# Hybrid decoder trunk: GpSimd issues the converting transfer of the next weight pair ahead of both subtracts of the present pair

## Chip, core and metric

The kernel runs on one core of one Trainium2 chip. The time is device microseconds of one execution. A profiled execution also gives a trace, whose span is a little shorter than the execution's time.

## What is computed

Two decoder layers act on x, 512 tokens by 2048 features, in float32. The part that matters here is the two large products of each layer:

```python
h = rms_norm(x, norm_g)
p = jnp.einsum('btd,dp->btp', h, w_in)          # 2048 x 7192
ya, yb, yc, yd = four mixers of slices of p     # GLA, window, differential, gated delta
y = jnp.concatenate([ya, yb, yc, yd], axis=-1)
return x + jnp.einsum('btm,md->btd', y, w_out)  # 2048 x 2048
```

The mixers are causal attention of four kinds, with 4 heads each, and a SiLU gate on each.

## The kernel before

**Split float32.** TensorE multiplies in a reduced float32 format (fp32r). To keep accuracy both factors are split into a high half (rounded to fp32r) and a low half (what is left), and three products are added: high by high, high by low, low by high (line 549).

**The weight stream.** All weights lie in DRAM as one stream of slices, each 128 rows by 512 columns, in the order in which they are used: 288 per layer, 576 in all. The trace and this text call the work on one slice a step (the code: kt). A step is 12 matmuls of 128x512: 4 accumulators by 3 products. Two slices make a pair; pair g holds steps 2g and 2g+1. There are 144 pairs per layer (`PAIRS`).

**Who makes what.** For each pair:

- SP's queue loads the raw float32 pair, 512 KB, into `w_raw`, 3 buffers deep (`RAW`, line 432). It may overwrite a buffer once both subtracts of the pair three before are done (line 431).
- GpSimd's queue loads the same pair a second time with a transfer that converts float32 to fp32r, into `w_hi`, 3 buffers deep (`HI`, `high_halves`, lines 477 to 482). It may overwrite a buffer once TensorE has done both steps of the pair three before (line 480). For the first 8 pairs (`FIRST_HI`) ScalarE makes the high halves instead, from `w_raw`.
- GpSimd subtracts, `w_lo = w_raw - w_hi`, one instruction for each step (line 506), into a ring of 4 `w_lo` buffers (`RING`). It waits for the buffer's last reader: the subtract of step n needs step n-4 done (line 505).
- TensorE waits before step n for its subtract, by the count `w_ready` (line 537), and counts `kt_done` after it (line 552). `kt_done` starts at 4.

GpSimd is one queue in order. Its loop (lines 484 to 509) takes for pair g: the wait for the raw pair, the wait for the high halves, the even subtract, then `high_halves(g + 1)` with its own wait, then the odd subtract. In pair 10 of the first layer it first converts masks (`masks`), and in the seventh pair of each layer it first scales some small weights (`small_weights`).

**TensorE's order.** `project` (line 525) runs the steps of one block of output columns and interleaves pieces of the mixers, so some steps follow each other directly and between others there are small matmuls. ScalarE and VectorE empty the accumulators (lines 1064, 1573, 1940) and do the mixers' elementwise work. At the end of a layer x, 4 MB, is written to DRAM in four transfers of 1 MB from ScalarE's queue (line 1472), while ScalarE (line 1084) and VectorE (lines 1521 to 1541) already prepare x for the next layer.

Of the kernel before, what the change touches and what calls it, by code (L numbers as in the profile page):

```python
# [16 lines left out]
DEPTH, SEQ, D_MODEL = 2, 512, 2048  # L17
# [22 lines left out]
PAIRS = LAYER_KTS // 2  # L40
RAW, HI, RING = 3, 3, 4
FIRST_HI = KT // 2
# [169 lines left out]
def hybrid_trunk(nc, x, wstream, wsmall, pcol, prow, wlr, cf, masks, out, rows):  # L212
    ctx = ExitStack()
    with ctx:
# [34 lines left out]
        def slot(n):  # L249
            return slots[:, n - FIRST_SLOT]  # L250
# [171 lines left out]
        @block.sync  # L422
        def _(sp):
            def x_in(n):
                k = X_PIECES[n]
                k = slice(k.start, k.stop)
                sp.dma_start(xT[:, k], x.rearrange("(k p) n -> p k n", p=P)[:, k]).then_inc(xin[n], 16)

            def weights(i):
                if i >= RAW:  # L430
                    sp.wait_ge(w_ready, 2 * (i - RAW) + 2)
                sp.dma_start(w_raw[:, i % RAW].rearrange("p a n -> p (a n)"),
                             wstream[i:i + 1].rearrange("a p n -> p (a n)")).then_inc(raw_in[i % RAW], 16)

            x_in(0)
            weights(0)
            x_in(1)
            weights(1)
            x_in(2)
            weights(2)  # L440
            x_in(3)
            for l in range(DEPTH):
                for i in range(PAIRS):
                    if l * PAIRS + i >= RAW:
                        weights(l * PAIRS + i)
                    if l == 0 and i in (RAW, RAW + 2):
                        x_in(4 + (i - RAW) // 2)
                    if i == RAW:
                        sp.wait_ge(ws_ready, l + 1)
                        if l:  # L450
                            sp.wait_ge(S_PE.sem, S_PE.at(l - 1, "small"))
                        sp.dma_start(ws[:, :], wsmall[l:l + 1].rearrange("a p n -> p (a n)")).then_inc(ws_in, 16)


        @block.gpsimd
        def _(pool):

            pool.sem_inc(ws_ready, 1)
            pool.memset(zeros[:, :], 0.0).then_inc(zeros_done, 1)

            def masks():

                pool.wait_ge(masks_in, 16)
                pool.wait_ge(consts_in, 16)
                pool.tensor_copy(mask_sb[:, 0:masks_n], slot(3).rearrange("p a b -> p (a b)")[:, 0:masks_n]) \
                    .then_inc(masks_done, 1)
                pool.tensor_copy(m_upto, upto).then_inc(masks_done, 1)

            def small_weights(l):

                each = ws[:, :].rearrange("p (k c) -> p k c", c=SM)
                pool.wait_ge(ws_in, l * 16 + 16)
                pool.wait_ge(norm_in, 16)
                pool.tensor_tensor(each, each, pcol_all[:, l, 0:KT].unsqueeze(2).broadcast_to([P, KT, SM]), ALU.mult) \
                    .then_inc(ws_ready, 1)

            def high_halves(g):

                if g >= HI:
                    pool.wait_ge(kt_done, RING + 2 * (g - HI) + 2)  # L480
                pool.dma_start(w_hi[:, g % HI].rearrange("p a n -> p (a n)"),  # L481
                               wstream[g:g + 1].rearrange("a p n -> p (a n)")).then_inc(hi_in[g % HI], 16)

            for l in range(DEPTH):
                for i in range(PAIRS):
                    g = l * PAIRS + i
                    if i == 10 and l == 0:
                        masks()
                    if i == 6:
                        small_weights(l)  # L490

                    pool.wait_ge(raw_in[g % RAW], g // RAW * 16 + 16)
                    if g >= FIRST_HI:
                        pool.wait_ge(hi_in[g % HI], len(range(FIRST_HI + (g - FIRST_HI) % HI, g + 1, HI)) * 16)
                    for k in range(2):
                        n = 2 * g + k

                        if n == 0:
                            continue
                        if n == 1:  # L500

                            pool.wait_ge(w_ready, 1)
                        if g < FIRST_HI:
                            pool.wait_ge(hi_made, n + 1)
                        pool.wait_ge(kt_done, n + 1)
                        pool.tensor_tensor(w_lo[:, n % RING], w_raw[:, g % RAW, k], w_hi[:, g % HI, k].bitcast(F32),  # L506
                                           ALU.subtract).then_inc(w_ready, 1)
                        if k == 0 and FIRST_HI <= g + 1 < DEPTH * PAIRS:
                            high_halves(g + 1)


        @block.tensor
# [1610 lines left out]
```

## Time and profile before

| | |
|---|---|
| median of 3 runs | 1834.73 us (1832.11 to 1838.42) |
| profiled execution | 1838.2 us |
| its span in the trace | 1836.1 us |
| TensorE matmul busy | 1817.9 us, 99% |
| GpSimd busy | 922.5 us, 50% |
| VectorE, ScalarE busy | 793.4 us, 511.2 us |
| moved by DMA | 324.98 MB, mean 177 GB/s |
| granted TensorE clock | 0.999 of full |

A busy share is an average over stages. What GpSimd's order of work is worth shows in where TensorE waits for a subtract, and in how far ahead of TensorE the subtracts end elsewhere.

### The profile page before, as it was taken

Reading aid. Unit: us, or ns where it says so; the run is one execution under the profiler, and the core shown is the slowest. Engines: PE = TensorE matmul, PEld = TensorE weight load, DVE = VectorE, ACT = ScalarE, POOL = GpSimd, SP = SyncE. Lnnn points to the kernel's source line nnn. Section 1 sums busy time; section 2 is a strip of 40 time slices with the busy share of each in tenths; the row PEclk is TensorE's granted clock in tenths of the full one; section 3 lists DMA queues with packets and bytes.
Section 4 is the critical chain, followed back from the end, with each engine's and each line's share of the span. In section 5 each row is a group of like instructions: output and inputs, shape, how many; then the busy total and the mean of one; then the engine's idle time right before and its main releaser. Section 6 shows DMA issues by size and latency. Waiting matters only on the chain. (4 is left out here: it accounts for less than half of the span.)

```text
span 1836.1 us, 23457 instructions
## 1 busy us (share of the span) xinstructions
PE 1817.9 (99%) x9462; PEld 1493.9 (81%) x9462; DVE 793.4 (43%) x1631; ACT 511.2 (28%) x991; POOL 922.5 (50%) x864
## 2 busy tenths in 40 slices
PE   8999999999999999999999999999999999999999
PEld 7788888888888888788877888888888888887887
DVE  7546634622111453643534476255311124436342
ACT  6212214022222543322312131140222225433220
POOL 5555544545555444445465555445455554444454
PEclk9999999999999999999999999999999999999999
DMA  7466554655555547455766665546555565474556
GB/s 276 144 191 209 169 161 138 185 151 171 176 171 179 162 146 240 139 158 173 242 207 183 188 205 171 159 142 182 156 170 178 161 180 164 139 242 134 161 173 206
DMA packets 94507, 324.98 MB, mean 177 GB/s; under 512 B 10144, under 2 KB 10688, under 8 KB 94144
## 3 DMA queue, kind: packets, MB, share of 16 engines
q1 hardware_dynamic: 43904, 155.73, 27.6%
q0 software_dynamic: 40320, 146.82, 27.1%
q10 hardware_dynamic: 10176, 20.94, 3.2%
q8 instruction: 74, 1.21, 0.3%
q14 instruction: 33, 0.27, 0.0%
HBM read 315.05 MB, written 8.40 MB: 176 GB/s over the span
## 5 line engine op out<-in xcount | busy, mean ns | idle before, releaser
L506 POOL TENSOR_TENSOR w_lo<-w_raw,w_hi 128x512 fp32r<-128x512 f32 x575 | 762.4, 1326 | 654.3 <-DMA w_hi<-in_wstream 471.4
L549 PE MATMUL acc<-w_hi,actT_hi 128*128 128x512 f32 x1408 | 561.8, 399 | 5.9 <-ACT slots L1064 5.9
L549 PE MATMUL acc<-w_hi,actT_lo 128*128 128x512 f32 x1408 | 549.2, 390 | 0.0
L549 PE MATMUL acc<-w_lo,actT_hi 128*128 128x512 f32 x1408 | 548.5, 390 | 0.0
L549 PE MATMUL acc<-actT_hi,w_hi 128*128 128x512 f32 x896 | 359.2, 401 | 6.8 <-DVE actT_lo L1521 3.2
L549 PE MATMUL acc<-actT_hi,w_lo 128*128 128x512 f32 x896 | 350.1, 391 | 0.0
L549 PE MATMUL acc<-actT_lo,w_hi 128*128 128x512 f32 x896 | 349.8, 390 | 0.0
L549 PEld LDWEIGHTS acc<-w_hi,actT_hi 128*128 128x128 f32 x1408 | 264.6, 188 | 62.3 <-ACT slots L1064 7.6
L549 PEld LDWEIGHTS acc<-w_hi,actT_lo 128*128 128x128 f32 x1408 | 264.3, 188 | 56.1
L549 PEld LDWEIGHTS acc<-w_lo,actT_hi 128*128 128x128 f32 x1408 | 264.7, 188 | 51.5
L481 POOL DMA_DIRECT2D w_hi<-in_wstream x280 | 159.2, 568 | 246.9 <-PE acc L549 242.7
L549 PEld LDWEIGHTS acc<-actT_hi,w_hi 128*128 128x128 f32 x896 | 168.6, 188 | 56.4 <-issue 18.9
L549 PEld LDWEIGHTS acc<-actT_hi,w_lo 128*128 128x128 f32 x896 | 168.6, 188 | 36.3
L549 PEld LDWEIGHTS acc<-actT_lo,w_hi 128*128 128x128 f32 x896 | 168.9, 189 | 32.6 <-issue 0.5
L1064 ACT ACTIVATE slots<-acc,xr 128x512 f32<-128x512 f32 x56 | 37.9, 690 | 172.1 <-PE acc L549 172.1
L1592 DVE SCALAR_TENSOR_TENSOR slots<-slots,pcol_all 128x511 f32<-128x511 f32 (+2 forms) x72 | 82.8, 1155 | 1.7
L1940 DVE TENSOR_TENSOR slots<-acc,slots 128x512 f32<-128x512 f32 x64 | 43.1, 690 | 87.9 <-PE acc L549 87.9
L1573 DVE TENSOR_TENSOR slots<-acc,slots 128x512 f32<-128x512 f32 x24 | 15.7, 688 | 131.9 <-PE acc L549 90.6
L1832 DVE SCALAR_TENSOR_TENSOR slots<-mix,slots 128x256 f32<-128x256 f32 x8 | 3.4, 424 | 133.1 <-ACT slots L1302 133.1
L598 PEld LDWEIGHTS mix<-slots 128*128 128x128 f32 x400 | 48.5, 191 | 2.0
L598 PE MATMUL mix<-slots 128*128 128x128 f32 x400 | 49.0, 275 | 0.0
L1931 DVE SCALAR_TENSOR_TENSOR actT_lo<-mix,pcol_all,actT_hi 128x512 fp32r<-128x512 f32 x32 | 22.4, 746 | 42.2 <-ACT actT_hi L1396 42.2
(270 smaller groups left out, 1558.7 us busy)
## 6 DMA issues: line engine op xcount, KB each, us to landing
w_raw<-in_wstream SPq DMA_DIRECT2D x288, 512.0 KB, 4.4
w_hi<-in_wstream POOLq DMA_DIRECT2D x280, 512.0 KB, 3.8
out_x<-slots ACTq DMA_DIRECT2D x7, 1024.0 KB, 7.5
slots<-in_x ACTq DMA_DIRECT2D x1, 4096.0 KB, 20.7
slots<-out_x ACTq DMA_DIRECT2D x1, 4096.0 KB, 18.4
slots<-in_x SPq DMA_DIRECT2D x3, 1024.0 KB, 12.8
slots<-rows ACTq DMA_DIRECT2D x2, 1024.0 KB, 6.0
out_x<-slots ACTq DMA_DIRECT2D x4, 256.0 KB, 2.1
```

The lines of the kernel that those rows point to most:

```text
L481: pool.dma_start(w_hi[:, g % HI].rearrange("p a n -> p (a n)"), wstream[g:g + 1].rearrange("a p n -> p (a n)")).then_inc(hi_in[g % HI], 16)
L506: pool.tensor_tensor(w_lo[:, n % RING], w_raw[:, g % RAW, k], w_hi[:, g % HI, k].bitcast(F32), ALU.subtract).then_inc(w_ready, 1)
L549: last = nc.tensor.matmul(acc[b][:, :], lhsT, rhs, start=(k == 0 and i == 0), stop=(k == kts - 1 and i == 2))
L598: last = nc.tensor.matmul(mh[bank][:, h], lhsT[:, h], rhs[:, h], start=True, stop=True)
L1064: nc.scalar.activation(slot(SLOT[c])[:, b], acc[b][:, :], ACT.Copy, scale=r) \
L1573: dve.tensor_tensor(slot(SLOT[c])[:, b], acc[b][:, :], rrow, ALU.mult).then_inc(acc_free, 1)
L1592: dve.scalar_tensor_tensor(dst[:, d:], src[:, 0:SEQ - d], tap[i], dst[:, d:], ALU.mult, ALU.add).then_inc(CONV_DVE.sem, CONV_DVE.one(f"{c} ...
L1832: dve.scalar_tensor_tensor(V["G"], mix[1][:, 0:256], 0.0, V["T0"], ALU.min, ALU.subtract) \
L1931: dve.scalar_tensor_tensor(actT_lo[:, k], mix[k % 4][:, :], pcv(l, PC["y"] + k), actT_hi[:, k].bitcast(F32), ALU.mult, ALU.subtract) \
L1940: dve.tensor_tensor(xs, acc[b][:, :], xs, ALU.add).then_inc(acc_free, 1)
```

## The change

The call that issues the converting transfer of pair g+1 moves from between the two subtracts of pair g to the front of the pair, ahead of the waits for the raw pair and the high halves of pair g. The function called is the same; its condition is the same but for `k == 0`, which has no meaning outside the inner loop.

```diff
                     if i == 6:
                         small_weights(l)
 
+                    if FIRST_HI <= g + 1 < DEPTH * PAIRS:
+                        high_halves(g + 1)
                     pool.wait_ge(raw_in[g % RAW], g // RAW * 16 + 16)
                     if g >= FIRST_HI:
                         pool.wait_ge(hi_in[g % HI], len(range(FIRST_HI + (g - FIRST_HI) % HI, g + 1, HI)) * 16)
...
                         pool.wait_ge(kt_done, n + 1)
                         pool.tensor_tensor(w_lo[:, n % RING], w_raw[:, g % RAW, k], w_hi[:, g % HI, k].bitcast(F32),
                                            ALU.subtract).then_inc(w_ready, 1)
-                        if k == 0 and FIRST_HI <= g + 1 < DEPTH * PAIRS:
-                            high_halves(g + 1)
```

## Rows read from the trace of the kernel before

**Rows 1.** The page: span, busy time of TensorE, and one line of its DMA issues.
```profile
span 1836.1 us, 23457 instructions
...
PE 1817.9 (99%) x9462; PEld 1493.9 (81%) x9462; DVE 793.4 (43%) x1631; ACT 511.2 (28%) x991; POOL 922.5 (50%) x864
...
w_raw<-in_wstream SPq DMA_DIRECT2D x288, 512.0 KB, 4.4
```

**Rows 2.** Waits of TensorE: who waited for whom, us in total, times, longest.
```profile
PE acc L549 <- ACT slots L1064: 5.9, 4, 1.7
PE acc L549 <- DVE actT_lo L1521: 3.2, 1, 3.2
PE acc L549 <- POOL w_lo L506: 2.5, 2, 1.6
```

**Rows 3.** Waits of GpSimd, same columns.
```profile
POOL w_lo L506 <- DMA w_hi<-in_wstream: 471.4, 222, 7.4
```

**Rows 4.** Lines 481 (issue) and 506 (subtract): duration min/median/max ns; landing of 481.
```profile
L481 POOL DMA_DIRECT2D w_hi<-in_wstream x280: 567/567/720, 39.9 to 1817.8; - x140
...
DMA to landing us min/median/max: 3.6/3.8/9.2
...
L506 POOL TENSOR_TENSOR w_lo<-w_raw,w_hi x575: 1263/1296/2627, 6.7 to 1823.0; 128x512 fp32r<-128x512 f32 x192
```

**Rows 5.** Timeline of GpSimd, first issue and steady stretch: start us, us, what, [idle before].
```profile
39.87 0.72 POOL L481 DMA_DIRECT2D w_hi<-in_wstream  x1
...
89.47 0.57 POOL L481 DMA_DIRECT2D w_hi<-in_wstream  x1 [0.24 <-PE acc L549]
90.06 1.30 POOL L506 TENSOR_TENSOR w_lo<-w_raw,w_hi 128x512 fp32r<-128x512 f32 x1
93.43 1.28 POOL L506 TENSOR_TENSOR w_lo<-w_raw,w_hi 128x512 fp32r<-128x512 f32 x1 [2.07 <-DMA w_hi<-in_wstream]
```

**Rows 6.** Timeline of TensorE, first matmul of steps 26 and 28.
```profile
89.01 0.39 PE L549 MATMUL acc<-actT_hi,w_hi 128*128 128x512 f32 x1
...
94.45 0.39 PE L549 MATMUL acc<-actT_hi,w_hi 128*128 128x512 f32 x1
```

**Rows 7.** Timeline of GpSimd at the layer boundary.
```profile
912.34 0.57 POOL L481 DMA_DIRECT2D w_hi<-in_wstream  x1
...
918.79 1.30 POOL L506 TENSOR_TENSOR w_lo<-w_raw,w_hi 128x512 fp32r<-128x512 f32 x1 [4.55 <-issue]
920.02 0.57 POOL L481 DMA_DIRECT2D w_hi<-in_wstream  x1
...
924.85 1.89 POOL L506 TENSOR_TENSOR w_lo<-w_raw,w_hi 128x512 fp32r<-128x512 f32 x1 [2.92 <-issue]
926.68 0.57 POOL L481 DMA_DIRECT2D w_hi<-in_wstream  x1
...
931.41 2.63 POOL L506 TENSOR_TENSOR w_lo<-w_raw,w_hi 128x512 fp32r<-128x512 f32 x1 [2.84 <-issue]
933.99 0.57 POOL L481 DMA_DIRECT2D w_hi<-in_wstream  x1
```

**Rows 8.** Timeline of TensorE there: last of step 287, first of 290, 292, 298.
```profile
919.67 0.39 PE L549 MATMUL acc<-actT_hi,w_lo 128*128 128x512 f32 x1
...
926.88 0.47 PE L549 MATMUL acc<-actT_hi,w_hi 128*128 128x512 f32 x1 [0.97 <-POOL w_lo L506]
...
934.19 0.47 PE L549 MATMUL acc<-actT_hi,w_hi 128*128 128x512 f32 x1 [1.58 <-POOL w_lo L506]
...
950.95 0.39 PE L549 MATMUL acc<-actT_hi,w_hi 128*128 128x512 f32 x1
```

**Rows 9.** Timeline of GpSimd around the longest landing.
```profile
705.82 0.57 POOL L481 DMA_DIRECT2D w_hi<-in_wstream  x1 [1.56 <-PE acc L549]
...
715.08 1.29 POOL L506 TENSOR_TENSOR w_lo<-w_raw,w_hi 128x512 fp32r<-128x512 f32 x1 [7.38 <-DMA w_hi<-in_wstream]
```

**Rows 10.** Busy time by window: the last columns are clock, DMA share, GB/s.
```profile
926.00:932.00 6.00, 5.12 (x23) 4.24 (x24) 5.97 (x7) 1.25 (x1) 3.14 (x4) 1.00 0.95 346
```

**Rows 11.** Timeline of VectorE at the boundary: one addition, twice.
```profile
915.96 0.69 DVE L1539 TENSOR_TENSOR slots<-slots 128x512 f32<-128x512 f32 x1
...
925.64 1.64 DVE L1539 TENSOR_TENSOR slots<-slots 128x512 f32<-128x512 f32 x1
```

## The prediction

> **What bounds the kernel now.** I read the busy shares first. TensorE is busy 1817.9 of the 1836.1 us span [rows 1]. No transfer and no other engine can be worth more than the 18 us that are left, unless it stretches TensorE's own work. So the next view is what TensorE waits for [rows 2]: ScalarE's copies out of the accumulators 5.9 us in 4 waits, VectorE's low half of x 3.2 us in one (the start, where x is still arriving), and GpSimd's `w_lo` 2.5 us in 2 waits. Only the last kind is touched by the change. GpSimd itself looks badly held up: its subtracts wait 471.4 us for the `w_hi` transfer [rows 3]. The question is how much of that reaches TensorE.
>
> Sizes: one issue of the converting transfer holds GpSimd 0.57 us, it lands after 3.8 us in the median and 9.2 us at most, and a subtract takes 1.30 us in the median and 2.63 at most [rows 4]. Call one 128x2048 slice of weights a step; TensorE takes 2g and 2g+1 from pair g. In a stretch without other work a pair takes 94.45 - 89.01 = 5.44 us of TensorE, a step 2.72 [rows 6].
>
> **The loop of before.** In such a stretch GpSimd issues the transfer at 89.47, 0.46 us after TensorE began a pair (89.01), subtracts the odd half at 90.06, idles about 2 us, and starts the next even subtract at 93.43 [rows 5, 6]. Issue to subtract is 3.96 us; with 1.28 us for the subtract, 5.24 us are gone, and only behind this subtract may the next transfer be issued. The loop (issue, landing, even subtract, next issue) is serial and has 5.44 - 5.24 = 0.2 us to spare. Any landing over about 4 us makes GpSimd fall behind by the excess. What protects TensorE is the ring of four `w_lo` buffers, a lead that takes several slow transfers to use up.
>
> Between the two layers that happens. The issues come at 912.34, 920.02, 926.68 and 933.99, thus 7.7, 6.7 and 7.3 us apart where TensorE wants 5.44; one landing takes 6.45 us (912.34 to 918.79), and one subtract takes 2.63 [rows 7]. TensorE then starts within 0.15 us of the end of an even subtract: at 926.88 and 934.19 after idles of 0.97 and 1.58 us [rows 8]. Those are the 2.5 us of [rows 2]; smaller hesitations and slower first matmuls after each wait are not in that figure. From the last matmul before step 288 (919.67) to the first of step 298 (950.95) pass 31.28 us; ten steps and one matmul pitch of 0.23 at full pace are 27.43. The loss there is 3.85 us.
>
> **The change, part by part.**
>
> *Moved: 280 issues.* None is added or removed; GpSimd still spends 280 x 0.57 us on them. The wait that comes with the issue of pair g+1 asks for step 2g-3 to be done. This is exactly what the odd subtract of pair g asks for. So where GpSimd is on time the transfer leaves at the same moment as before, 0.46 us after TensorE starts step 2g-2, and lands no earlier. The gain can only be where GpSimd was late.
>
> *Moved behind that wait: the even subtract.* It needed only step 2g-4; now it starts a step later. New timetable from the start of step 2g-2: issue at 0.46, even subtract 1.05 to 2.35, odd subtract to 3.65. TensorE needs the even one at 5.44, so 3.1 us are spare in place of a lead of two to three steps; the odd one is needed at 8.16, with 4.5 spare. With the longest subtract seen, 2.63 [rows 4], the even one still ends at 3.7. Cost: none, covered by TensorE's two steps. If that cover were gone, every microsecond over would be paid per pair.
>
> *Removed: the serial loop.* The transfer of pair g now has from 0.46 after step 2g-4 to about 1.05 after step 2g-2, thus 6.0 us, before it delays GpSimd at all, and until 10.88 - 0.46 - 1.30 = 9.1 us before TensorE waits. The layer boundary's 6.45 is under that by 2.7 us, and still by 1.3 with the 2.63 us subtract. The only landings of 9.2 us are near 705.82, where GpSimd idles 7.38 [rows 9], and the same stretch of the second layer; TensorE has mixer matmuls between its steps there and did not wait for `w_lo` before. There the timing is the same or better, since the following issue no longer stands behind the late one. Gain: between the 2.5 us that the waits list [rows 2] and the 3.85 us of elapsed time; I take the elapsed time, because the slow restarts go with the waits.
>
> *SP's queue.* The next raw load is released by the odd subtract, which ends 1.3 us later than before (3.65 in place of 2.35). It takes 4.4 us in the median [rows 1], so it lands at 8.1, and is first read three pairs later, at 16.32 + 1.05. Nothing waits.
>
> *Start, masks, small weights.* The first moved transfer was issued at 39.87 with GpSimd busy right before it [rows 5]; now it comes before the subtracts of steps 14 and 15. TensorE waits there for x (the 3.2 us of [rows 2]), so step 14 has some 6 us in hand. The masks and the scaling of the small weights stay ahead of the issue; the latter, in pair 150, falls into the 1.8 us that GpSimd has free per pair (5.44 - 3.65). No cost.
>
> *Bandwidth.* In the boundary stretch two `w_hi` transfers may now be in flight. The weight streams at full pace ask for 2 x 512 KB per 5.44 us, 193 GB/s. In the worst 6 us the engines were 95% busy at 346 GB/s [rows 10]. A load landing a little later costs nothing until 9.1 us.
>
> **Sum.** -3.85 us, rounded -3.9. The profiled execution was 1838.2 us, span 1836.1; it becomes 1834.3. It was 3.5 us above the median of the three runs; against that median, 1834.73, the forecast is 1830.9, or 0.21% less. A measurement of this kernel tells about 0.3% (5.5 us) from no change; the three runs of before alone span 0.34%.
>
> **Rivals.**
>
> A. *The time is not kept.* TensorE arrives earlier and then waits as much longer for ScalarE or VectorE, where it already waits 5.9 us [rows 2]. For: those waits exist in the second layer. Against: ScalarE and VectorE get their work from the accumulators, so they move with TensorE. Time 1834.7, chance 0.14. A program whose order makes no difference at all falls here too.
>
> B. *Back-to-back subtracts hold VectorE.* The same VectorE addition takes 0.69 us at 915.96 and 1.64 at 925.64, where it lies beside a subtract; that subtract is slow as well [rows 7, 11]. Before, two subtracts were separated by the issue and the landing; now they form one block of 2.6 us, and a VectorE addition behind it could wait 1.3 us more. It matters where TensorE waits for such a chain: 4 waits on ScalarE and about one more. 5 x 1.3 = 6.5, so 1830.9 + 6.5 = 1837.4. Against: the number of overlaps does not grow, only their grouping, and TensorE hides nearly all. Chance 0.08. The Trainium skill, "SBUF — State Buffer", section "SBUF: two separate sides", speaks against the change here: VectorE and GpSimd share a port pair that one instruction locks whole. By that rule the long times are one engine waiting out the other's instruction, and the time would be B's 1837.4; by the rows it is 1830.9, because few such waits end at TensorE.
>
> C. *Slower.* In the boundary the second `w_hi` transfer in flight takes bandwidth from the first, and landings double, 2 x 6.45 = 12.9. Then two pairs take 0.46 + 12.9 + 1.30 = 14.66 us, 7.33 per pair, 1.89 over TensorE's pace, for the 8 pairs in which the four write-backs of x run: 15.1 us. 1830.9 + 15.1 = 1846.0. It decides only from a landing of 9.1 us. For: 95% busy engines in one stretch [rows 10]. Against: the issues stay tied to TensorE's steps, so total demand rises by no more than the recovered stall. Chance 0.04.
>
> **Numbers.** The forecast has 0.74. Its 0.21% lies near the 0.3% bound, so measurement scatter puts about a fifth of it beyond: faster 0.15. A and B lie within the bound; C and scatter of B give slower 0.06; same 0.79. The range reaches from 1827.0 (forecast less scatter) through A to B, 1837.5; C is left out.
>
> **What would show it.** Right: no TensorE wait on `w_lo` between 915 and 950; steps 288 to 298 in 27.4 to 27.6 us; GpSimd in steady stretches as issue, subtract, subtract, with issues still 0.46 us after TensorE's step; its idle mostly on TensorE and no longer on the transfer; median landing still near 3.8. Wrong: even subtracts ending less than 1 us before their step, TensorE's waits on ScalarE or VectorE grown by what left `w_lo` (A), longer VectorE additions (B), landings over 9 us at the boundary (C).

## The result, and the profile after

The change made the kernel slower: 1850.48 us (median of 6, 1848.9 to 1853.63) against 1835.6 us (1832.11 to 1840.27, 6 runs). The ratio is 1.0081, with a 95% interval of 1.0066 to 1.0096. The forecast was 1830.9 with a range up to 1837.5. One of the eleven executions of run 11 below took 2012.46 us at a granted clock of 0.851; the ratio given there leaves it out.

The page of the changed kernel. In line 508, the subtract, the last number is GpSimd's idle time ahead of it:

```profile
span 1851.5 us, 23457 instructions
...
PE 1822.0 (98%) x9462; PEld 1494.5 (81%) x9462; DVE 844.8 (46%) x1631; ACT 511.4 (28%) x991; POOL 902.4 (49%) x864
...
L508 POOL TENSOR_TENSOR w_lo<-w_raw,w_hi 128x512 fp32r<-128x512 f32 x575 | 739.5, 1311 | 28.7 <-issue 8.7
```

TensorE's work is the same to 4 us, and GpSimd waits 1.5 us for its transfer ahead of a subtract, in place of 471.4 [rows 3]. But VectorE, whose program nobody touched, is busy 51 us longer than in [rows 1]. What TensorE waits for, against [rows 2]:

```profile
PE mix L719 <- DVE halves L1837: 8.4, 8, 1.0
PE acc L549 <- ACT slots L1064: 5.9, 4, 1.7
PE mix L592 <- DVE slots L1677: 3.6, 1, 3.6
PE mix L712 <- DVE slots L1669: 1.8, 2, 0.9
...
PE mix L948 <- DVE slots L1541: 1.4, 1, 1.4
PE mix L865 <- DVE slots L2021: 1.3, 2, 0.7
```

The wait on `w_lo` is gone and the one on ScalarE is unchanged. All that is new is waits for VectorE, at matmuls of the mixers and, at the start, at those that sum the squares of x (line 948). Its instructions by line, first before and then after (count | busy us, mean ns):

```profile
L1592 DVE SCALAR_TENSOR_TENSOR slots<-slots,pcol_all 128x511 f32<-128x511 f32 (+2 forms) x72 | 82.8, 1155 | 1.7
...
L1837 DVE TENSOR_TENSOR halves<-slots,halves 128x256 fp32r<-128x256 f32 x8 | 14.7, 1841 | 0.3
...
L1634 DVE TENSOR_TENSOR glog<-glog,stat 128x16 f32<-128x16 f32 x2 | 0.4, 176 | 0.1
```

```profile
L1592 DVE SCALAR_TENSOR_TENSOR slots<-slots,pcol_all 128x511 f32<-128x511 f32 (+2 forms) x72 | 97.6, 1360 | 1.7
...
L1837 DVE TENSOR_TENSOR halves<-slots,halves 128x256 fp32r<-128x256 f32 x8 | 24.5, 3056 | 0.3
...
L1634 DVE TENSOR_TENSOR glog<-glog,stat 128x16 f32<-128x16 f32 x2 | 6.0, 3024 | 0.1
```

A subtraction of 16 columns went from 0.18 to 3.02 us. It does not compute longer; it is held. The timeline shows by what. Line 1837 makes the low half of the logs in the second mixer (gated linear attention), and TensorE's line 719 needs it. Before, and then after, first GpSimd's rows and then VectorE's:

```profile
420.33 0.57 POOL L481 DMA_DIRECT2D w_hi<-in_wstream  x1 [0.83 <-PE acc L549]
420.92 1.30 POOL L506 TENSOR_TENSOR w_lo<-w_raw,w_hi 128x512 fp32r<-128x512 f32 x1
...
420.69 1.83 DVE L1837 TENSOR_TENSOR halves<-slots,halves 128x256 fp32r<-128x256 f32 x1
```

```profile
425.17 0.57 POOL L481 DMA_DIRECT2D w_hi<-in_wstream  x1 [3.99 <-PE acc L549]
425.76 2.52 POOL L508 TENSOR_TENSOR w_lo<-w_raw,w_hi 128x512 fp32r<-128x512 f32 x2
...
425.52 3.06 DVE L1837 TENSOR_TENSOR halves<-slots,halves 128x256 fp32r<-128x256 f32 x1
```

Before, line 1837 ends 0.3 us after one subtract (422.52 against 422.22); after, 0.3 us after two (428.58 against 428.28). VectorE already lost one subtract here in the kernel before. But it ended in time for TensorE in seven tiles of eight. In the eighth (at 1478.38) the even subtract came late and held the copy of line 1835 ahead of it as well (1.08 us for 0.29), and TensorE waited 0.7 us.

At the start the same thing happens once. VectorE's addition of line 1541 took 0.69 us before (at 46.53). After, it lies beside two subtracts, and the matmuls of line 948, ahead of step 15, wait for it:

```profile
45.86 2.52 POOL L508 TENSOR_TENSOR w_lo<-w_raw,w_hi 128x512 fp32r<-128x512 f32 x2
...
45.56 3.38 DVE L1541 TENSOR_TENSOR slots<-slots 128x512 f32<-128x512 f32 x1
```

The steps of the two traces can be laid beside each other: the start of each step's first matmul after, less that before, and the steps at which this difference changes.

| stretch | change, us |
|---|---|
| start, to step 13 | -5.05 |
| steps 15, 16 (line 948) | +3.25 |
| step 59, behind the convolutions | +5.35 |
| steps 131, 133, 149, 165, 181 and 419, 421, 437, 453, 469 (gated linear attention) | +11.3 |
| steps 196, 484 (window attention) | +1.1 |
| steps 235, 252, 523, 540 (differential attention) | +2.9 |
| steps 288 to 296, layer boundary | -3.4 |
| sum | +15.4 |

This is the difference of the spans, 1851.5 - 1836.1. The first row belongs to the execution of before: TensorE waited 3.2 us there [rows 2]. The boundary run (run 11), with the same order at the start, lost only 0.8 us in place of 5.0 between steps 11 and 14.

Three of these losses are larger than the wait in them, because behind the wait the granted TensorE clock was half of full, 1.2 in place of 2.4 GHz. The rows have TensorE's busy time first and the granted clock third from the end: first before (behind the wait of 3.2 us), then twice after (behind the waits of 1.4 us at line 948 and of 3.6 us at step 59):

```profile
42.80:46.20 3.40, 3.40 (x8) 2.70 (x9) 3.37 (x5) 0.88 (x1) 0.00 (x0) 0.50 0.81 264
...
49.60:53.00 3.40, 3.40 (x10) 2.17 (x10) 0.00 (x0) 0.66 (x2) 0.00 (x0) 0.51 0.37 142
182.70:186.10 3.40, 3.40 (x13) 2.91 (x12) 1.39 (x5) 3.16 (x7) 0.00 (x0) 0.51 0.44 154
```

3.4 us at half the clock are 1.7 us of work not done. The +5.35 of step 59 is thus a wait of 3.6 us and 1.7 us of clock. No such stretch follows the waits of about 1.2 us in gated linear attention.

The boundary went as forecast: the last matmul before step 288 and the first of step 298, 27.42 us apart (31.28 in [rows 8]). These 3.9 us include small drifts that the table's row does not count.

```profile
931.52 0.39 PE L549 MATMUL acc<-actT_hi,w_lo 128*128 128x512 f32 x1
...
958.94 0.39 PE L549 MATMUL acc<-actT_hi,w_hi 128*128 128x512 f32 x1
```

So the question for the experiments is about the 23.9 us that the other rows add: is it that the subtracts are joined, where they lie, or the transfers?

### The profile page after: what moved, and what is told of

It reads as the page before. It is cut to its first block, busy times and chain, and to the rows that moved or that the text cites. A ratio compares the mean times of both kernels' runs of the same rounds, so it can differ in the third digit from the quotient of the medians.

```text
span 1851.5 us, 23457 instructions
## 1 busy us (share of the span) xinstructions
PE 1822.0 (98%) x9462; PEld 1494.5 (81%) x9462; DVE 844.8 (46%) x1631; ACT 511.4 (28%) x991; POOL 902.4 (49%) x864
## 4 chain that ended last, share of the span: by engine, by line
PE 88%; DVE 6%; ACT 4%; DMA 1%; issue 0%; ACTq 0%; SPq 0%; DVEq 0%
PE acc L549 75%; PE mix L598 2%; DVE halves L1837 1%; DVE slots L1592 1%; DMA w_raw<-in_wstream 1%; ACT slots L1064 1%; PE mix L855 1%; PE mix L965 1%; PE mix L784 1%; PE mix L809 1%; PE mix L874 1%; ACT L1302 1%; PE mix L592 1%; DMA slots<-rows 0%; DVE slots L1669 0%
## 5 line engine op out<-in xcount | busy, mean ns | idle before, releaser
L508 POOL TENSOR_TENSOR w_lo<-w_raw,w_hi 128x512 fp32r<-128x512 f32 x575 | 739.5, 1311 | 28.7 <-issue 8.7
L1592 DVE SCALAR_TENSOR_TENSOR slots<-slots,pcol_all 128x511 f32<-128x511 f32 (+2 forms) x72 | 97.6, 1360 | 1.7
L1164 ACT ACTIVATE general<-slots 128x512 f32<-128x512 f32 x24 | 15.2, 634 | 99.5 <-DVE slots L1592 99.5
```

The costliest lines, as they stand in the source:

```text
L1592: dve.scalar_tensor_tensor(dst[:, d:], src[:, 0:SEQ - d], tap[i], dst[:, d:], ALU.mult, ALU.add).then_inc(CONV_DVE.sem, CONV_DVE.one(f"{c} ...
```

## Experiments

Edits are shown against the kernel named. Ratios are to the kernel before, run on the same chip.

**1. The odd subtract one step later** (`e1`), against the changed kernel:

```diff
-                        pool.wait_ge(kt_done, n + 1)
+                        pool.wait_ge(kt_done, n + 1 + (k if g >= FIRST_HI else 0))
```

> The changed kernel, but the odd subtract waits for one more step of TensorE, so that it starts 2.7 us after the even one and about 0.85 us lie free between them. Theory 1 (block: two subtracts back to back hold a VectorE instruction with two SBUF inputs through both, 1837 took 3.06 us in place of 1.83): line 1837 falls back to about 1.84 us, TensorE's waits on VectorE vanish, the layer boundary's gain of 3.4 us stays: 1832 to 1838 us. Theory 2 (place: what hurts is that the even subtract now lies right behind the start of an even step, where the mixers' VectorE chains begin, joined or not): 1843 to 1851. Theory 3 (transfers: the later raw load and transfer order delay the small transfers, such as the rows of log decays that landed 4.7 us later): 1850, no change.

Measured: 1830.78 us, ratio 0.9971 (0.996 to 0.9982). Line 1837 took 1.84 us in the mean, and no mixer's matmul waits for VectorE (line 518 is the warm-up at the start). The transfers are out as a cause, since their order is that of the changed kernel and the raw loads are released later still, and so is the place of the even subtract by itself, which is unchanged. The time is a little below the range of theory 1 (1832 to 1838).

```profile
PE acc L549 <- ACT slots L1064: 5.9, 4, 1.7
PE mix L518 <- DVE smT L1487: 1.5, 1, 1.5
PE acc L549 <- issue: 0.6, 1, 0.6
```

**2. A gap of one semaphore** (`e2`), against the changed kernel:

```diff
                         pool.wait_ge(kt_done, n + 1)
+                        if k and g >= FIRST_HI:
+                            pool.wait_ge(w_ready, n)
```

> The changed kernel, but the odd subtract waits for the completion of the even one, so that only a gap of one semaphore, about 0.1 us, lies between them; places in time are otherwise those of the changed kernel. Theory 1: if a waiting VectorE instruction takes the port in such a gap, 1834 to 1840 with line 1837 near 1.84 us; if not, 1850. Theory 2 and theory 3: 1850 to 1852, since neither the places nor the transfers move.

Measured: 1831.79 us, ratio 0.9981 (0.9971 to 0.9992). The two subtracts take 2.74 us together in place of 2.52, at the same place in the step, and that is enough for VectorE to get in between (line 1837 is 1839 in this kernel). The time is 2 us below theory 1's range:

```profile
416.81 2.74 POOL L510 TENSOR_TENSOR w_lo<-w_raw,w_hi 128x512 fp32r<-128x512 f32 x2
...
416.57 1.83 DVE L1839 TENSOR_TENSOR halves<-slots,halves 128x256 fp32r<-128x256 f32 x1
```

One wait of GpSimd on its own completion turns 0.8% slower into 0.2% faster. Nothing else differs from the changed kernel.

**3. A joined subtract in the old order** (`e3`), against the kernel before (the declarations of `spare` and `spare_done` are left out here, and the subtract into `w_lo` is cut short):

```diff
+                        if k and g >= FIRST_HI:
+                            if g > FIRST_HI:
+                                pool.wait_ge(spare_done, g - FIRST_HI)
+                            pool.tensor_tensor(spare[:, :], w_raw[:, g % RAW, k],
+                                               w_hi[:, g % HI, k].bitcast(F32), ALU.subtract).then_inc(spare_done, 1)
                         pool.tensor_tensor(w_lo[:, n % RING], ...
```

> The kernel before, with one more subtract of the same inputs, written to a spare bfloat16 tile, right ahead of each odd subtract: a block of 2.6 us in place of 1.3 us, with the order of the transfers as before. Nothing of the computation is left out. Theory 1: 15.4 us as in the changed kernel plus the 3.4 us that it gained at the boundary, and some more because the even subtract stays apart as a third: 1850 to 1858, line 1837 at about 3.1 us. Theory 2: at most a few us, 1836 to 1841, since the even subtract keeps its place. Theory 3: 1835.6, no change but some at the boundary, where GpSimd is late.

Measured: 1878.48 us, ratio 1.0239 (1.0224 to 1.0254). Line 1837 (here 1844) took 3.07 us, and the waits in gated linear attention are, in the first layer, those of the changed kernel to 0.01 us (1.18, 1.22, 1.23, 1.22, 1.23). So two joined subtracts are enough, without any of the change. The size was missed by 20 us. GpSimd subtracts 364 us more, and the convolutions and the first mixer (gated delta) lose 24 us, at steps 57, 79, 345, 367 and 368. Of the span's 38 us over the kernel before about 12 are clock. Behind idles of 2.1 to 5.3 us four stretches, 23.8 us together, ran at half the granted clock, and TensorE is busy 1829.9 us in place of 1817.9. The row by itself below is one of these stretches. Two idles of TensorE at line 652, 6.6 us together, the profile puts down to nothing that it shows; they were not taken apart.

```profile
PE mix L599 <- DVE slots L1612: 9.8, 2, 5.3
PE mix L726 <- DVE halves L1844: 9.4, 8, 2.1
PE mix L652 <- issue: 6.6, 2, 3.3
...
PE acc L556 <- POOL w_lo L513: 1.8, 1, 1.8
```

```profile
1103.20:1110.00 6.80, 5.60 (x20) 4.96 (x21) 3.60 (x12) 2.71 (x6) 0.07 (x1) 0.50 0.61 231
```

**4. Both subtracts later, still joined** (`e6`), against the changed kernel:

```diff
-                        pool.wait_ge(kt_done, n + 1)
+                        pool.wait_ge(kt_done, n + 1 + (2 - k if g >= FIRST_HI else 0))
```

> The changed kernel, but both subtracts wait for one more step of TensorE (two more than the even one needs): the same joined block of 2.6 us, 2.2 us later against TensorE's steps. Theory 1: chains hit by it lose as much, but partly other chains: 1843 to 1858. Theory 2: the mixers' chains are past: 1832 to 1840, the boundary gain kept. Theory 3: 1850. In this run the even subtract ends only about 0.9 us before its step, so TensorE may wait for w_lo where a subtract is slow; the wait on w_lo says how much of the time that is.

Measured: 1830.46 us, ratio 0.9975 (0.9965 to 0.9986). This refuted theory 1 as it stood: the block is as long as in the changed kernel, 2.53 us, and costs nothing. It has moved past line 1837, and now holds line 1841, for which TensorE does not wait:

```profile
L1841 DVE SCALAR_TENSOR_TENSOR slots<-slots 128x256 f32<-128x256 f32 x8 | 12.2, 1524 | 24.9 <-ACT slots L1306 24.9
...
L1837 DVE TENSOR_TENSOR halves<-slots,halves 128x256 fp32r<-128x256 f32 x8 | 3.4, 427 | 0.3
```

Mended theory: the cost needs both, a joined block and a chain that TensorE waits for under it. As both GpSimd's issue and the mixers' chains start at fixed points of TensorE's steps, they meet in every tile or in none.

**5. The issue between the two** (`f1`), against the kernel before:

```diff
-                        pool.wait_ge(kt_done, n + 1)
+                        pool.wait_ge(kt_done, n + 1 + (1 - k if g >= FIRST_HI else 0))
```

> The kernel before, with one edit: the even subtract waits for one more step, the same that the issue and the odd subtract wait for. The order stays even subtract, issue, odd subtract, with the 0.57 us of the issue between the two subtracts, all right behind the start of an even step. Theory 1 as mended by the first four runs (a cost only where the two subtracts touch AND a VectorE instruction that TensorE waits for falls on them): the issue separates them, 1830 to 1833 us, line 1837 near 1.84 us, no TensorE wait on VectorE. Rival, the place alone: 1843 to 1851. Rival, the issue itself holds VectorE's port like a subtract: line 1837 over 3.5 us and 1855 or more.

Measured: 1848.5 us, ratio 1.0064 (1.004 to 1.0088); the expectation was wrong, and the time is the one named for the rival "place alone". The chain in this kernel, VectorE's rows and then GpSimd's:

```profile
416.64 1.28 DVE L1835 CAST halves<-slots 128x256 fp32r<-128x256 f32 x1
417.96 1.93 DVE L1837 TENSOR_TENSOR halves<-slots,halves 128x256 fp32r<-128x256 f32 x1
...
416.49 1.28 POOL L506 TENSOR_TENSOR w_lo<-w_raw,w_hi 128x512 fp32r<-128x512 f32 x1 [2.31 <-PE acc L549]
417.72 0.57 POOL L481 DMA_DIRECT2D w_hi<-in_wstream  x1
418.31 1.28 POOL L506 TENSOR_TENSOR w_lo<-w_raw,w_hi 128x512 fp32r<-128x512 f32 x1
```

The copy of line 1835 (0.29 us when free) is held by the even subtract, and line 1837 by the odd one. The subtracts do not touch, yet the chain loses both. Joined or not is thus not the last word. What counts is how much subtract time falls on a chain: TensorE's slack covers one, not two. For the changed kernel the place alone is excluded by runs 1 and 2, whose even subtract starts 1.06 us behind the step's start as in the changed kernel, at no cost. Here it starts at 0.34 us, and no run has that place with the odd subtract off the chain. In run 2 the gap lets line 1837 through between them, and the chain loses one. The recorded start of line 1837 is 0.35 us ahead of the odd subtract here, during the issue, and it needs 0.43 us; whether the issue held it as well is open. Here TensorE also waits 5.0 us for `w_lo` (7 waits), since the even subtract is late and the loop is still serial.

**6 to 8. The joined order in parts.** The kernel of run 2 everywhere but in the pairs named, where the gap is left out:

```diff
-                        if k and g >= FIRST_HI:
+                        if k and g >= FIRST_HI and i not in range(64, 96):
```

with `range(16, 30)` in the second, and in the third the gap only in both ranges.

> The kernel of the run e2 (odd subtract waits for the even one's completion, 1831.8 us), with the subtracts joined again, as in the changed kernel, only in pairs 64 to 95 of each layer, where the second mixer (gated linear attention) runs. Theory 1, mended: the waits of TensorE on line 1837 come back, 5 of 1.2 us in each layer: 12.1 us, 1842.5 to 1845.5. Rival, a cost spread over all pairs (lead, transfers): 64 of 280 pairs, a quarter of 19 us: 1835 to 1837.

> The kernel of the run e2, with the subtracts joined only in pairs 16 to 29 of each layer, where VectorE works on the convolutions and the small transfer of log decays goes out and comes back. Theory 1, mended: the one wait of 5.35 us before step 59 comes back in the first layer and none in the second: 1835 to 1839. Rival, cost spread over all pairs: 28 of 280 pairs: 1833 to 1834.5. Rival, the late landing of the log decays was chance of that execution: 1831 to 1833.

> The kernel of the run e2, with the subtracts joined everywhere but in pairs 16 to 29 and 64 to 95 of each layer (188 of 280 pairs). Theory 1, mended: only the small waits of the window and differential attention come back, about 1.2 us in each layer: 1833 to 1836. Rival, cost spread over all pairs: 188 of 280, two thirds of 19 us: 1843 to 1846.

Measured: gated linear attention 1843.25 us, ratio 1.0037 (1.0024 to 1.005), with the ten waits of the changed kernel back at the same steps; convolutions 1841.01, 1.0020 (1.0007 to 1.0034); the rest 1837.61, 0.9999 (0.9986 to 1.0012). Against run 2's 0.9981 these are 0.56%, 0.39% and 0.18%, or 10.3, 7.2 and 3.3 us, together 20.8. The changed kernel lies 1.00% over run 2, 18.4 us. By the intervals of the ratios each of these has about 3 us of uncertainty. So the cost adds up by place, and the third part, with 188 of 280 pairs, has the least of it: the rival of an evenly spread cost falls.

Two of the three expectations missed. The convolutions cost more in the times than expected, and less in their profile (1.35 us at step 59, and 2.07 at step 347 in the second layer). The profiled execution took 1836.0 us, the fastest of ten and the only one with a mean granted clock of 1.000; the other nine had 0.998 or 0.999 and took 1837.8 to 1845.0. In this profile no stretch of halved clock follows the waits, in that of the changed kernel one does.

The rest came out above its 1833 to 1836. Its profile is 5.8 us longer than run 2's: 2.8 of them at steps 15 and 16, where line 1541 is held for 3.39 us as in the changed kernel, and 2.2 in differential attention. The start is a place that the theory did not name.

**9, 10. The convolutions, one layer each**, `g not in range(16, 30)` and `g - PAIRS not in range(16, 30)` in the same place:

> The kernel of the run e2, subtracts joined only in pairs 16 to 29 of the first layer. The run with both layers lay 9 us over e2 in its times and only 3.4 us in its profile, with waits at steps 59 and 347. Theory (VectorE's convolution is held, ScalarE issues the return of the log decays about 2 us later, and its landing of 7 to 9 us in place of 6.5 ends late, by an amount that changes from run to run): a part of the cost in each layer, 1834 to 1838 here, with more scatter than e2's 4 us, and the issue of the return at 167 us in place of 165.15. Rival (only the first layer, which is behind from the start, pays): all of it here, 1839 to 1841.

> The same for pairs 16 to 29 of the second layer alone. Theory: 1834 to 1838, with the issue of the return of the log decays about 2 to 3 us later than e2's 1074.0 and TensorE's wait before step 347. Rival (only the first layer pays): 1831 to 1833.

Measured: 1834.79 us (1831.17 to 1839.29), ratio 0.9994 (0.9978 to 1.0009), and 1835.31 (1832.66 to 1839.05), 0.9996 (0.9984 to 1.0007). Against run 2 that is about 2.4 and 2.8 us, each with an interval of about 3 us to both sides, so the times alone do not show that both layers pay. The profiles do: step 59 loses 4.6 us in the first, step 347 1.5 us in the second. The chain, first in run 2 and then with the first layer joined: ScalarE's issue of the transfer that brings the log decays back, and in the second case also VectorE's wait for it.

```profile
165.15 0.35 ACTq L1203 DMA_DIRECT2D slots<-rows  x1
```

```profile
168.31 0.35 ACTq L1203 DMA_DIRECT2D slots<-rows  x1
...
163.35 4.92 DVE L1594 SCALAR_TENSOR_TENSOR slots<-slots,pcol_all 128x511 f32<-128x511 f32 x3
...
176.81 2.67 DVE L1600 TENSOR_SCALAR slots<-slots,glog 128x128 f32<-128x128 f32 x8 [6.08 <-DMA slots<-rows]
```

The three taps take 4.92 us. ScalarE's last activation of the convolution waits for them, and the return of the decays is issued behind it, at 168.31 here. It lands 8.5 us later, where run 2's took 6.5. TensorE loses 4.6 us at step 59: it waits 3.1 us, and then the granted clock is half of full from about 181.2 to 184.6. The landing took between 4.3 and 9.0 us in the profiles of these kernels. Why it differs was not taken apart. It fits the wider scatter of the times, and so does the clock behind the longer waits.

**11. The boundary alone** (`g2`), against the kernel before: the new order in pairs 138 to 151, the old one elsewhere.

```diff
+                    first = g in range(138, 152)
+                    if first and FIRST_HI <= g + 1 < DEPTH * PAIRS:
+                        high_halves(g + 1)
...
-                        if k == 0 and FIRST_HI <= g + 1 < DEPTH * PAIRS:
+                        if k == 0 and not first and FIRST_HI <= g + 1 < DEPTH * PAIRS:
```

> The kernel before, with the new order in pairs 138 to 151 alone, around the boundary of the layers. Theory (the part of the prediction that held: the serial loop is opened there, TensorE's waits on w_lo at steps 288 to 296 go, and no chain of the mixers is hit in these pairs): 3.4 us faster than before, 1831 to 1834, and the steps from 287 to 298 at full pace. Rival (the waits come back in another place, or the gain is in the joined order's effect elsewhere): within 1 us of before.

Measured: 1831.43 us, ratio 0.9980 (0.997 to 0.9989): 3.7 us faster, 2.0 to 5.5 by the interval. No wait on `w_lo` is left; in its place TensorE waits 0.4 us for one of VectorE's additions of line 1940.

**12. The start alone** (`g1`): the same edit with `first = g == FIRST_HI - 1`.

> The kernel before, with the new order in pair 7 alone, the first pair that has an issue. In the profiles of before and after, the new order keeps GpSimd from joining a third subtract to the two of pair 6 there, and the wait of 3.15 us that TensorE had for line 1521 at step 12 is gone. Theory (the same port, with the other sign: three joined subtracts held VectorE's sums ahead of the low half of x): 2 to 4 us faster than before, 1831 to 1834. Rival (the start differs by chance, with the arrival of x): no change from before.

Measured: 1833.55 us against 1835.24, ratio 0.9996 (0.9986 to 1.0005): no difference that can be told. In its profile the first issue comes after an idle of 3.3 us, in place of a third joined subtract, and the wait of TensorE for x at step 12 is 0.2 us. But it was 0.6 us at the longest in the boundary run as well, whose start is that of the kernel before. The 3.15 us in the profile of before is mostly chance of that execution, and the -5.05 us in the table cannot be credited to the change.

## Why the prediction was wrong

**The bound and the loop: right.** TensorE has no other bound. In a steady stretch GpSimd issues 0.47 us after TensorE's step starts (87.69 against 87.22), then subtracts twice, then waits for TensorE, as the timetable said:

```profile
87.69 0.57 POOL L481 DMA_DIRECT2D w_hi<-in_wstream  x1 [2.31 <-PE acc L549]
88.28 2.54 POOL L508 TENSOR_TENSOR w_lo<-w_raw,w_hi 128x512 fp32r<-128x512 f32 x2
```

**The removed loop: right, and its size.** 3.85 us forecast; 3.9 in the profile (31.28 - 27.42), 3.7 in the times of the boundary run, with a wide interval.

**"Moved behind that wait: the even subtract. ... Cost: none, covered by TensorE's two steps": this step failed.** It counted the lead of `w_lo` over TensorE, which indeed held: TensorE does not wait for `w_lo` once. It did not count the other thing that a subtract does, hold VectorE. In gated linear attention the even subtract started 2.5 us ahead of line 1837 before and 0.24 us behind its start after. So it moved by 2.7 us onto the chain on which the odd one already lay, in every tile, and elsewhere onto ScalarE's issue of the log decays through the convolution. In place of nothing this cost 23.9 us in the profile, and 18.4 us in the times of the changed kernel against run 2. The part on the start, the masks and the small weights ("No cost.") failed the same way: 3.25 us of it lie at steps 15 and 16.

**Rival B had the mechanism and was mis-sized: 6.5 us forecast, 23.9 in the profile.** Its price multiplied 1.3 us by the places where TensorE waited before, about 5, on ScalarE. But those four waits stayed at 5.9 us; the cost came at 19 steps, and at 18 of them the profile of before has no wait for VectorE, because the slack there covered one subtract. No term of the prediction had the halved clock behind a long wait either, 1.7 us each at steps 15 and 16 and at step 59. The place to look was not TensorE's waits but VectorE's lengthened instructions: line 1837 had a mean of 1.84 us for 256 columns before, in eight of eight cases. The argument against B, "the number of overlaps does not grow, only their grouping", missed that the grouping is what exceeds the slack. The other argument, that TensorE hides nearly all, was true for one subtract and false for two.

The rule of the Trainium skill ("SBUF — State Buffer", "SBUF: two separate sides") agrees with the traces here, where the forecast went by the rows of waits: an instruction of the other engine holds the port pair for its whole length, and line 1837 took 1.83 us beside one subtract. What the page says of one instruction the trace shows of two in a row, 3.06 us. That a copy with a single SBUF input is held as well (1.28 for 0.29 us, run 5) fits the page's other case, an instruction in a two-port mode; no run here tests which mode it was in. The page says that whichever engine starts first gets the pair. By the recorded starts VectorE began 0.24 us ahead of the subtract that held it (425.52 and 425.76); what the two engines ask for in between the trace does not show.

**Rivals A and C: did not occur.** ScalarE's waits stayed the same, and the largest landing stayed 9.2 us.

**The chances.** B had 0.08 and a time within the range. A better estimate from the trace of before would have taken the lengthened instructions one by one: eight of line 1837 with 1.3 us each less an unknown slack, 0 to 10 us. That alone reaches from the forecast, 1830.9, to well above the kernel before.

## What to carry to other kernels

Where one engine's instructions hold another's, as GpSimd's subtracts hold VectorE here, an instruction moved on one engine is also a hold moved on the other: look in the trace for the other engine's instructions that take longer than their shape needs, and ask what a second hold there would meet. Long instructions that are ready together should be kept apart by a wait, for the neighbour's sake: here a wait on the own completion gave 1831.79 in place of 1850.48 us. With it the issue ahead of both subtracts is a gain, and the odd or both subtracts one step later have the lowest times found, 1830.78 and 1830.46 us against 1835.68 for the kernel before. Their ratios, 0.9971 and 0.9975, are not told apart from run 2's 0.9981 or from the 0.9980 of the new order at the boundary alone.

## Not expected of the hardware

- Two GpSimd subtracts that follow each other without a wait left VectorE no chance in between: held for 3.06 us by two subtracts of 2.52 us together. A wait on a semaphore that the first one itself raises lengthens the pair to 2.74 us and opens it: 1.83 us.
- A VectorE subtraction of 16 columns took 0.18 us free and 3.02 us in the mean beside two subtracts.
- An issue of a converting transfer between two subtracts (0.57 us) did not protect a chain of two VectorE instructions: each met a subtract, 1.28 and 1.93 us.
- A wait of TensorE can cost more than its length: behind waits of 1.4 and 3.6 us the granted clock was 0.51 for 3.4 us, and matmuls of 0.39 us took 0.59 to 0.77.
